# A two-layer streaming encoder step: the first two tiles of the pool projection taken together, and what is moved around them

## The chip, the cores and the metric

The kernel runs on one core of a Trainium2 chip. The time is the device time in microseconds (us) of one execution. Engines are named as in the profile: PE (TensorE, matmuls; PEld its weight loads), DVE (VectorE), ACT (ScalarE), POOL (GpSimd), SP (SyncE, which issues most DMA transfers).

## What is computed

Two layers over 512 prompt rows and 32 sample rows (544 rows, kept as columns), width 2048, all in fp32. Layer 0 is attention; the change touches its last stage and the whole of layer 1, the pool mixer:

```python
mod = (cond @ w_ada[i] + b_ada[i])[:, None, :]        # cond = silu(c)
shift, scale, gate = jnp.split(mod, 3, axis=-1)
h = _rmsnorm(x, g_norm[i]) * (1 + scale) + shift
...
u, gate = jnp.split(h @ w_in, 2, axis=-1)             # the pool projection, 2048 -> 4096
u_ext = jnp.concatenate([prefix, u], axis=1)
# four channel groups: trailing means over 2, 4, 8, 16 rows, minus u  -> d
m = einsum(d, w_grp) * scale
y = (m * jax.nn.silu(gate)) @ w_out
x = x + gate_mod * y
```

## The kernel before

**Tiles.** A projection is done in tiles of 128 output channels. A tile's weights are 128 x 2048 fp32 (1 MB). They are loaded into one of two slots of `w_raw`, and DVE splits them in two instructions into an upper part `w_hi` (L1607) and a lower part `w_lo` (L1608); this is `split(g)`, for the tile with the running number g. PE multiplies upper by upper, upper by lower, and lower by upper part of `h`, 16 blocks of 128 input channels, each block three products on two halves of the 544 columns: 96 matmuls of 272 columns a tile, accumulated in the PSUM slot `g % 2` (two banks). Tile g may be split when tile g-2 has been multiplied, and its raw weights may be loaded when tile g-2 has been split. `big_wait` is PE's wait for the split and for the free PSUM slot, `big_tile` the 96 matmuls.

**Pool projection.** There are 32 such tiles, `G_PIN` to `G_PIN + 31`, called pool tile 0 to 31 here. Even ones give 128 channels of `u`, odd ones the matching gate channels. `u_and_gate(t)` on ACT evicts tile 2t into `u_ext`, and tile 2t+1 through silu to `stage` and to DRAM. DVE forms the trailing means of tile 2t in between (L2015 and the lines behind it, here the pool work), and ACT stores them (`d_scr`).

**Modulation on DVE.** The vector `cond @ w_ada` is made partly by DVE: `ada_tile(a)` multiplies a 1 MB tile of `w_ada` with the broadcast condition `cond_b` (two instructions L1645) and counts `adr_used`. Sixteen of these tiles (modulation tile 0 to 15 here) are left for the pool projection: one per pool tile in the loops t = 0 to 7. They all go through one buffer, `w_adr[:, 1]`, so SP may load modulation tile k only when tile k-1 has been used. SP works in order, and its instructions are waits and issues: for each t it issued the weights of pool tiles 2t and 2t+1, and then modulation tiles 2t and 2t+1 (L641 to L646).

**Between the layers.** The last tiles of the attention's output projection (`G_O2 + 14`, `G_O2 + 15`) go PE, ACT (`gated`: eviction L1510, then square L1203), DVE (`update` L1976, x + gate * y), POOL (L715, sum of squares). After the last one PE sums over the partitions (`row_sums(1)`), DVE and ACT make 1/rms (`row_scale`, L1582, L1587, L1209), and `make_h1` on DVE with `affine1` on ACT makes the 16 blocks of `h` (L1618, L1231, L1626), one after the other; `h_ready` counts them. PE took pool tile 0 block by block as they came (`big_tile` with `h_wait`), and then tile 1. ACT made `silu` of `cond_b` (L1525) behind `affine1`, and DVE's loop starts with a wait for it, and then `split(G_PIN + 1 + 2t)`.

**Loop of DVE before**, for each t: split of tile 2t+1, modulation tile 2t, pool work, split of tile 2t+2, modulation tile 2t+1, a wait for the store of the means. After t = 15 comes the group stage (`G_GRP`, four 512 x 512 maps) and the last projection (`G_POUT`).

## Time and profile before

| | us |
|---|---|
| median of 3 runs | 2057.33 (2054.09 to 2057.75) |
| the profiled execution, its time | 2055.34 |
| its span | 2053.6 |
| PE busy | 1842.7 (90%) |
| DVE busy | 1257.0 (61%) |
| ACT busy | 413.7 (20%) |
| mean granted TensorE clock | 0.944 of full speed |

The times of the trace count from the start of the span, of which 1.7 us of the execution's time lie outside. The trace lists consecutive instructions of one form as one row; "idle before" in square brackets is what the engine waited before the row, and for whom.

### The profile page before, as it was taken

To read this page: it belongs to the slowest core of one execution; us is meant where nothing else is said; L and a number is where in the kernel's file an instruction comes from. 1 tells how busy PE (TensorE), PEld (TensorE's weight loads), DVE (VectorE), ACT (ScalarE), POOL (GpSimd) and SP (SyncE) were. 2 spreads that over 40 slices of the span, in tenths; PEclk is the share of its full clock that TensorE was granted. 3 is DMA by queue.
4 is the path that set the end of the run, shared out by engine and by line. 5 is a ranking of instruction groups with operands and counts; after the bars stand their busy time and mean duration, and the time that the engine had idled before them with its cause. 6 is when DMAs were issued, how large, how long until landed. Compare 5 with 4: busy or idle time off the path is not lost.

```text
span 2053.6 us, 32706 instructions
## 1 busy us (share of the span) xinstructions
PE 1842.7 (90%) x13182; PEld 1702.1 (83%) x13182; DVE 1257.0 (61%) x1601; ACT 413.7 (20%) x914; POOL 198.1 (10%) x117
## 2 busy tenths in 40 slices
PE   4548999999999999997888889959999999999995
PEld 0108999999999997776777779958999999999995
DVE  4898766776876674553555544377777544574444
ACT  1241000000010113331455533440000000121111
POOL 2770000000600000000000011200000000001110
PEclk8878999999999999999799998979999999999997
DMA  9664554554655532205333253304455332552222
GB/s 387 233 225 175 203 208 185 206 210 185 234 192 211 193 135 62 75 15 164 99 117 117 87 207 128 96 37 169 182 185 202 118 113 103 179 186 82 82 82 87
DMA packets 86106, 316.07 MB, mean 154 GB/s; under 512 B 12184, under 2 KB 20552, under 8 KB 60448
## 3 DMA queue, kind: packets, MB, share of 16 engines
q1 hardware_dynamic: 64208, 237.70, 32.0%
q10 hardware_dynamic: 21200, 76.48, 10.4%
q0 software_dynamic: 640, 1.10, 0.2%
q8 instruction: 38, 0.62, 0.1%
q14 instruction: 20, 0.16, 0.0%
HBM read 282.56 MB, written 32.69 MB: 154 GB/s over the span
## 4 chain that ended last, share of the span: by engine, by line
PE 69%; DVE 12%; DMA 6%; issue 5%; ACT 4%; POOL 2%; SPq 0%; DVEq 0%; ACTq 0%; POOLq 0%
PE banks L732 68%; DVE banks L1645 3%; DMA w_raw<-in_w_pin 3%; POOL ssq L690 2%; DMA w_adr<-in_w_ada_dve 2%; DMA w_more<-in_w_ada_pe 2%; ACT pxd L1428 1%; DVE std L1884 1%; DVE w_hi L1607 1%; DVE h_lo L400 1%; DVE rstd L1587 1%; DVE x L2083 1%; ACT px L1346 0%; DVE pt_lo L1818 0%; DVE w_hi L1868 0%
## 5 line engine op out<-in xcount | busy, mean ns | idle before, releaser
L732 PE MATMUL banks<-h_hi,w_hi 128*128 128x272 f32 x3968 | 831.4, 295 | 61.2 <-DVE w_lo L1608 29.6
L732 PE MATMUL banks<-h_lo,w_hi 128*128 128x272 f32 x3712 | 778.3, 292 | 0.0
L732 PE MATMUL banks<-h_hi,w_lo 128*128 128x272 f32 x3456 | 722.8, 291 | 0.0
L732 PEld LDWEIGHTS banks<-h_hi,w_hi 128*128 128x128 f32 x3968 | 635.4, 194 | 70.3 <-issue 47.8
L732 PEld LDWEIGHTS banks<-h_lo,w_hi 128*128 128x128 f32 x3712 | 596.5, 193 | 0.0
L732 PEld LDWEIGHTS banks<-h_hi,w_lo 128*128 128x128 f32 x3456 | 547.6, 192 | 0.0
L1645 DVE CUSTOM_DVE_ANT_0 banks<-w_adr,cond_b 128x2048 f32<-128x2048 f32 x160 | 386.2, 2414 | 20.2 <-DMA w_adr<-in_w_ada_dve 17.0
L1607 DVE CAST w_hi<-w_raw 128x2048 fp32r<-128x2048 f32 x101 | 125.6, 1244 | 223.4 <-PE banks L732 171.5
L1608 DVE TENSOR_TENSOR w_lo<-w_raw,w_hi 128x2048 fp32r<-128x2048 f32 x101 | 249.2, 2467 | 3.5
L1280 ACT ACTIVATE stage<-banks 128x544 f32<-128x544 f32 x46 | 28.9, 629 | 495.6 <-PE banks L732 495.6
L1976 DVE TENSOR_TENSOR x<-x,stage 128x544 f32 (+1 forms) x32 | 23.9, 748 | 171.0 <-ACT stage L1510 171.0
L715 POOL TENSOR_TENSOR ssq<-ssq,stage 128x544 f32<-128x544 f32 x32 | 49.9, 1560 | 751.0 <-ACT stage L1203 751.0
L732 PE MATMUL banks<-w_more,cond_t 128*2 128x512 f32 x80 | 40.6, 661 | 38.1 <-DMA w_more<-in_w_ada_pe 21.2
L1510 ACT ACTIVATE stage<-banks,mod 128x272 f32<-128x272 f32 (+2 forms) x96 | 32.6, 410 | 202.3 <-PE banks L732 202.3
L732 PEld LDWEIGHTS banks<-w_more,cond_t 128*2 128x2 f32 x80 | 6.7, 90 | 70.6 <-issue 44.0
L732 PE MATMUL banks<-w_raw,cond_t 128*2 128x512 f32 x48 | 31.2, 812 | 32.8 <-DMA w_raw<-in_w_ada_pe 32.8
L2015 DVE TENSOR_TENSOR w<-u_ext 128x573 f32<-128x573 f32 x16 | 12.1, 756 | 69.6 <-ACT u_ext L1535 68.6
L732 PEld LDWEIGHTS banks<-w_raw,cond_t 128*2 128x2 f32 x48 | 4.5, 103 | 57.8 <-DMA w_raw<-in_w_ada_pe 30.5
L1540 ACT ACTIVATE stage<-banks 128x544 f32<-128x544 f32 x16 | 10.0, 626 | 186.6 <-PE banks L732 186.6
L1428 ACT ACTIVATE pxd<-banks,std 128x128 f32<-128x128 f32 (+3 forms) x64 | 33.2, 524 | 64.8 <-DVE std L1885 41.0
L721 POOL TENSOR_TENSOR cos_t<-cos_t,kpe 128x544 f32<-128x544 f32 x8 | 10.8, 1346 | 343.4 <-ACT kpe L1400 343.4
L1932 DVE TENSOR_TENSOR ptd_lo<-banks,ptd_hi 128x128 fp32r<-128x128 f32 (+3 forms) x32 | 15.7, 492 | 43.3 <-ACT ptd_hi L1450 43.3
(301 smaller groups left out, 1703.8 us busy)
## 6 DMA issues: line engine op xcount, KB each, us to landing
w_adr<-in_w_ada_dve ACTq DMA_DIRECT2D x46, 1024.0 KB, 4.9
w_adr<-in_w_ada_dve SPq DMA_DIRECT2D x34, 1024.0 KB, 4.9
w_raw<-in_w_z SPq DMA_DIRECT2D x32, 1024.0 KB, 5.9
w_raw<-in_w_pin SPq DMA_DIRECT2D x32, 1024.0 KB, 5.9
w_raw<-in_w_gate SPq DMA_DIRECT2D x16, 1024.0 KB, 7.0
w_raw<-in_w_out SPq DMA_DIRECT2D x32, 512.0 KB, 3.9
w_raw<-in_w_pout SPq DMA_DIRECT2D x16, 1024.0 KB, 4.9
w_more<-in_w_ada_pe SPq DMA_DIRECT2D x10, 1024.0 KB, 7.4
```

Of the source, the lines that this page charges most:

```text
L400: ins = eng.scalar_tensor_tensor(out=h_lo[:, k, r], in0=x[:, k, r], scalar=mod[:, c, k:k + 1], in1=h_hi[:, k, r].bitcast(F32), op0=ALU.add ...
L690: pool.tensor_tensor(ssq[:], ssq[:], (stage[:, 0], rstd[:])[k % 2], ALU.add).then_inc(sq_added, 1)
L715: pool.tensor_tensor(ssq[:], ssq[:], stage[:, s], ALU.add).then_inc(sq_added, 1)
L732: return pe.matmul(out, lhsT, rhs, start=start, stop=stop)
L1280: act.activation(rows(stage[:, s]), acc[slot], func).then_inc(acc_free[slot], 1)
L1428: ins = act.activation(pxd[:, w % 3, e, 0:n], PS[:, 2 * (w % 2) + e, 0:n], ACT.Exp, bias=std[:, w, 2 + e:3 + e], scale=DIFF_SCALE, accum_o ...
L1510: ins = act.activation(stage[:, s, r], PS[:, 2 * slot + bank, cols], ACT.Identity, scale=mod[:, c, bass.ds(2 * t + (gate_tile + s), 1)])
L1587: vchain(dve, dve.reciprocal(rstd[:], rstd[:]))
L1607: vchain(dve, dve.tensor_copy(w_hi[:, slot], w_raw[:, slot]))
L1608: dve.tensor_tensor(w_lo[:, slot], w_raw[:, slot], w_hi[:, slot].bitcast(F32), ALU.subtract).then_inc(split_ready, 1)
L1645: ins = dve.tensor_tensor_reduce(ada_junk, w_adr[:, slot if buf is None else buf], cond_b[:, c, :], 1.0, 0.0, ALU.mult, ALU.add, ada_acc[: ...
L1976: dve.tensor_tensor(at(x, t2 + k), at(x, t2 + k), stage[:, slot], ALU.add).then_inc(x_new, 1)
```

## The change

PE takes pool tiles 0 and 1 together: for each of the 16 blocks of `h` the products of tile 0 and then of tile 1. For this the weights of tile 1 are split earlier, between `fold_scale` and `row_scale`. All later splits of DVE's loop move by one tile: at t it now splits tile 2t+2 first, and tile 2t+3 behind the pool work; the last two of these (t = 15) are the weights of groups 0 and 1, and the group stage splits one group further ahead. SP loads the weights of pool tiles 0 and 1 first and then, for each t, modulation tile 2t, weights of tile 2t+2, modulation tile 2t+1, weights of tile 2t+3. The silu of `cond_b` stands on ACT ahead of the last two `gated` steps of the attention instead of behind `affine1`. The first tile of layer 0 (`G_KPE`) is only written out, with the same instructions.

```diff
--- before.py
+++ after.py
@@ -638,13 +638,14 @@
                     sp.wait_ge(split_ready, 2 * t + 2 + G_O2 - G_KPE + s)
                     sp.dma_start(w_raw[:, (G_O2 + s) % 2, 0:D // 2],
                                  tile_of(wo2, s, t + 1)[:, 0:D // 2]).then_inc(raw_in[(G_O2 + s) % 2], 16)
+            for s in range(2):
+                load_w(w_pin[s], (G_PIN + s) % 2, G_PIN - G_KPE + s)
             with sp.Fori(0, KT // 2) as t:
-                for s in range(2):
-                    load_w(tile_of(wp2, s, t), (G_PIN + s) % 2, 2 * t + G_PIN - G_KPE + s)
                 for s in range(2):
                     sp.wait_ge(adr_used, 2 * t + (ADA_P0 + ADA_P1 + s))
                     sp.dma_start(w_adr[:, 1], tile_of(wd2, s, t + (ADA_P0 + ADA_P1) // 2)).then_inc(adr_in[s], 16)
-            with sp.Fori(KT // 2, KT) as t:
+                    load_w(tile_of(wp2, s, t + 1), (G_PIN + s) % 2, 2 * t + G_PIN + 2 - G_KPE + s)
+            with sp.Fori(KT // 2 + 1, KT) as t:
                 for s in range(2):
                     load_w(tile_of(wp2, s, t), (G_PIN + s) % 2, 2 * t + G_PIN - G_KPE + s)
             sp.wait_ge(adr_used, ADA_P0 + ADA_P1 + KT)
@@ -778,10 +779,8 @@
                                   first and i == 0, last and i == 2)
                 return m
 
-            def big_tile(slot, h_wait=None):
+            def big_tile(slot):
                 for k in range(KT):
-                    if h_wait is not None:
-                        pe.wait_ge(h_ready, h_wait + k + 3)
                     m = tile_products(slot, k, k == 0, k == KT - 1)
                 m.then_inc(mm_done, 1)
 
@@ -800,7 +799,10 @@
             ada_turn(CHUNKS - 1)
 
             big_wait(G_KPE)
-            big_tile(G_KPE % 2, 0)
+            for k in range(KT):
+                pe.wait_ge(h_ready, k + 3)
+                m = tile_products(G_KPE % 2, k, k == 0, k == KT - 1)
+            m.then_inc(mm_done, 1)
             big_loop(G_Z, 0, ZT // 2)
             big_loop(G_GATE, 0, GT // 2 - 1)
             big_wait(G_GATE + GT - 2)
@@ -1153,7 +1155,12 @@
             row_sums(1)
             for s in range(2):
                 big_wait(G_PIN + s)
-                big_tile((G_PIN + s) % 2, KT)
+            for k in range(KT):
+                pe.wait_ge(h_ready, KT + k + 3)
+                for s in range(2):
+                    m = tile_products((G_PIN + s) % 2, k, k == 0, k == KT - 1)
+                    if k == KT - 1:
+                        m.then_inc(mm_done, 1)
             big_loop(G_PIN, 1, KT)
             for g in range(4):
                 slot = (G_GRP + g) % 2
@@ -1517,12 +1524,12 @@
 
             with act.Fori(0, KT // 2 - 1) as t:
                 gated(t, G_O2, 1, 2 * KT, halves=True)
+            act.wait_ge(condb_in, 32)
+            act.activation(cond_b[:], cond_b[:], ACT.Silu).then_inc(condb_ready, 1)
             with act.Fori(KT // 2 - 1, KT // 2) as t:
                 gated(t, G_O2, 1, 2 * KT)
             root(1)
             affine1()
-            act.wait_ge(condb_in, 32)
-            act.activation(cond_b[:], cond_b[:], ACT.Silu).then_inc(condb_ready, 1)
 
 
             act.wait_ge(pad_zero, 1)
@@ -1991,6 +1998,7 @@
                     split(G_PIN)
             dve.memset(lam_in[:, 0, 0:1], 0.0).then_inc(pad_free, 1)
             fold_scale(1)
+            split(G_PIN + 1)
             row_scale(1)
             make_h1()
 
@@ -2003,7 +2011,7 @@
                     t0 = t - 4 * grp
                     dv.loop(t0, 2 + grp + 1 + 1 + 1 + (4 if grp < 2 else 0))
                     dve_t2 = 2 * t
-                    split(G_PIN + 1, dve_t2, t)
+                    split(G_PIN + 2, dve_t2, t)
                     if grp < 2:
                         ada_tile(ADA_P0 + ADA_P1, dve_t2, t, 1)
                     dve.wait_ge(acc_free[us], t + turn_of(G_PIN + 2))
@@ -2025,7 +2033,7 @@
                     dve.tensor_copy(last[:, 0, :], u_ext[:, NP:PAD + NP])
                     vchain(dve, dve.tensor_copy(last[:, 1, :], u_ext[:, PAD + R:2 * PAD + R]))
                     dve.memset(lam_in[:, 0, 0:1], 0.0).then_inc(d_ready, 1)
-                    split(G_PIN + 2, dve_t2, t)
+                    split(G_PIN + 3, dve_t2, t)
                     if grp < 2:
                         ada_tile(ADA_P0 + ADA_P1 + 1, dve_t2, t, 1)
                     dve.wait_ge(d_stored, 16 * t + 16)
@@ -2059,12 +2067,13 @@
             lower_d(0)
             dve.wait_ge(pg_stored, 16 * KT)
             for g in range(4):
-                split(G_GRP + g + 1)
                 group_out(4 * g)
                 if g < 3:
                     lower_d(g + 1)
                 for n in range(1, 4):
                     group_out(4 * g + n)
+                if g < 3:
+                    split(G_GRP + g + 2)
                 dve.memset(lam_in[:, 0, 0:1], 0.0).then_inc(acc_free[(G_GRP + g) % 2], 1)
             group_out(KT)
 
```

On SP's queue, in the loop over the first eight t, this stood before (a repetition issues two weight tiles, then two modulation tiles):

```order
L641 ISA
L482 ISA [waits split_ready]
L482 DMA w_raw<-in_w_pin 128x2048
L481 REGISTER_ALU
L482 ISA [waits split_ready]
L482 DMA w_raw<-in_w_pin 128x2048
L645 REGISTER_ALU
L646 ISA [waits adr_used]
L646 DMA w_adr<-in_w_ada_dve 128x2048
L645 REGISTER_ALU
L646 ISA [waits adr_used]
L646 DMA w_adr<-in_w_ada_dve 128x2048
```

and this stands there now:

```order
L646 ISA [waits adr_used]
L646 DMA w_adr<-in_w_ada_dve 128x2048
L481 REGISTER_ALU
L482 ISA [waits split_ready]
L482 DMA w_raw<-in_w_pin 128x2048
L645 REGISTER_ALU
L646 ISA [waits adr_used]
L646 DMA w_adr<-in_w_ada_dve 128x2048
L481 REGISTER_ALU
L482 ISA [waits split_ready]
L482 DMA w_raw<-in_w_pin 128x2048
L643 REGISTER_ALU
```

Each of the two weight issues now stands behind a wait on `adr_used` of its own. On DVE, at the end of the attention, this stood before (the last `update` steps, `pad_free`, `fold_scale`, `row_scale`):

```order
L1976 TENSOR_TENSOR x<-x,stage 128x544 [waits acc_free1]
L1607 CAST w_hi<-w_raw 128x2048 [waits mm_done,raw_in1]
L1608 TENSOR_TENSOR w_lo<-w_raw,w_hi 128x2048 [waits dve_step]
L1976 TENSOR_TENSOR x<-x,stage 128x544 [waits acc_free0]
L1992 MEMSET lam_in 128x1
L1598 SCALAR_TENSOR_TENSOR aff<-mod,gnorm_t 128x16 x2
L1582 TENSOR_SCALAR rstd<-banks 128x544 [waits var_ready,dve_step]
```

and this stands there now:

```order
L1983 TENSOR_TENSOR x<-x,stage 128x544 [waits acc_free1]
L1614 CAST w_hi<-w_raw 128x2048 [waits mm_done,raw_in1]
L1615 TENSOR_TENSOR w_lo<-w_raw,w_hi 128x2048 [waits dve_step]
L1983 TENSOR_TENSOR x<-x,stage 128x544 [waits acc_free0]
L1999 MEMSET lam_in 128x1
L1605 SCALAR_TENSOR_TENSOR aff<-mod,gnorm_t 128x16 x2
L1614 CAST w_hi<-w_raw 128x2048 [waits mm_done,raw_in0,dve_step]
L1615 TENSOR_TENSOR w_lo<-w_raw,w_hi 128x2048 [waits dve_step]
L1589 TENSOR_SCALAR rstd<-banks 128x544 [waits var_ready]
```

The split of tile 1 has come in ahead of the instruction that reads the row sums. On ACT this stands now between the loop of `gated` and its last two steps (a table load and the silu, which were behind `affine1`), and a table load for the square root has come in behind them:

```order
L1528 ACT_TABLE_LOAD
L1528 ACTIVATE cond_b<-cond_b 128x4096
L1529 UNCONDITIONAL_BRANCH
L1517 ACTIVATE stage<-banks,mod 128x272
L1517 ACTIVATE stage<-banks,mod 128x240
```

The silu now stands ahead of the evictions of the attention's last two tiles. The loop of `u_and_gate`, which had no table load before, now has one ahead of the copy of `pool_pre` (L1538) and one ahead of the silu of the gate tile (L1547).

## Rows read from the trace of the kernel before

**Rows 1.** The page: the chain that ended last, shares of the span by engine.

```profile
PE 69%; DVE 12%; DMA 6%; issue 5%; ACT 4%; POOL 2%; SPq 0%; DVEq 0%; ACTq 0%; POOLq 0%
```

**Rows 2.** Waits of PE, 1240 to 1700 us: us in total, times, longest.

```profile
PE banks L732 <- DVE w_lo L1608: 17.9, 8, 5.3
```

**Rows 3.** Timeline of PE: start us, us, instruction, idle before.

```profile
1356.34 0.79 PE L732 MATMUL banks<-h_hi,w_hi 128*128 128x272 f32 x2 [9.09 <-DVE h_lo L1626]
...
1382.02 0.41 PE L732 MATMUL banks<-h_hi,w_lo 128*128 128x272 f32 x2
1387.69 0.82 PE L732 MATMUL banks<-h_hi,w_hi 128*128 128x272 f32 x2 [5.26 <-DVE w_lo L1608]
...
1404.03 0.52 PE L732 MATMUL banks<-h_hi,w_hi 128*128 128x272 f32 x2 [2.16 <-DVE w_lo L1608]
```

**Rows 4.** Timeline of DVE between the layers.

```profile
1338.08 3.34 DVE L1608 TENSOR_TENSOR w_lo<-w_raw,w_hi 128x2048 fp32r<-128x2048 f32 x1
1342.19 0.73 DVE L1976 TENSOR_TENSOR x<-x,stage 128x544 f32<-128x544 f32 x1 [0.77 <-ACT stage L1510]
...
1347.36 0.72 DVE L1582 TENSOR_SCALAR rstd<-banks 128x544 f32<-128x544 f32 x1 [4.26 <-PE banks L732]
...
1378.34 1.74 DVE L1626 SCALAR_TENSOR_TENSOR h_lo<-w,mod,h_hi 128x512 f32 x4
```

**Rows 5.** Timeline of POOL between the layers.

```profile
1337.68 1.59 POOL L715 TENSOR_TENSOR ssq<-ssq,stage 128x544 f32<-128x544 f32 x1 [3.94 <-ACT stage L1203]
1343.68 1.33 POOL L715 TENSOR_TENSOR ssq<-ssq,stage 128x544 f32<-128x544 f32 x1 [4.41 <-ACT stage L1203]
```

**Rows 6.** Timeline of ACT between the layers.

```profile
1331.20 0.66 ACT L1203 ACTIVATE stage<-x 128x544 f32 x1
1335.13 1.02 ACT L1510 ACTIVATE stage<-banks,mod 128x272 f32<-128x272 f32 x3 [3.27 <-PE banks L732]
...
1378.78 1.28 ACT L1525 ACT_TABLE_LOAD   x1
1380.07 3.62 ACT L1525 ACTIVATE cond_b<-cond_b 128x4096 f32<-128x4096 f32 x1
```

**Rows 7.** Timeline of DVE in the loop, t = 1: modulation, pool work, split, modulation.

```profile
1417.04 2.30 DVE L1645 CUSTOM_DVE_ANT_0 banks<-w_adr,cond_b 128x2048 f32<-128x2048 f32 x1
...
1427.38 1.23 DVE L1607 CAST w_hi<-w_raw 128x2048 fp32r<-128x2048 f32 x1 [5.28 <-DMA w_raw<-in_w_pin]
...
1433.24 2.30 DVE L1645 CUSTOM_DVE_ANT_0 banks<-w_adr,cond_b 128x2048 f32<-128x2048 f32 x1
```

**Rows 8.** The casts L1607, 1415 to 1600 us: what DVE waited for before them.

```profile
  DMA w_raw<-in_w_pin: 34.6, 7
```

**Rows 9.** Timeline of SP's DMA issues: weights of pool tiles 4 and 5, modulation tile 4.

```profile
1420.42 0.91 SPq L482 DMA_DIRECT2D w_raw<-in_w_pin  x2
1435.78 0.33 SPq L646 DMA_DIRECT2D w_adr<-in_w_ada_dve  x1
```

**Rows 10.** Modulation loads, 1400 to 1600 us: issue to landing, us.

```profile
DMA to landing us min/median/max: 4.8/4.9/5.9
```

**Rows 11.** Stretches: PE, PEld, DVE, ACT, POOL busy, then clock, DMA share, GB/s.

```profile
1421.50:1429.50 8.00, 8.00 (x66) 8.00 (x65) 2.58 (x7) 0.00 (x0) 0.00 (x0) 1.00 0.99 399
1387.60:1392.00 4.40, 4.31 (x19) 4.31 (x20) 4.37 (x4) 0.00 (x0) 0.00 (x0) 0.51 0.02 4
```

**Rows 12.** Timeline of ACT: evictions as pool tiles 2, 17 and 31 end.

```profile
1417.87 0.75 ACT L1535 ACTIVATE u_ext<-banks 128x272 f32<-128x272 f32 x3 [12.53 <-PE banks L732]
...
1612.12 0.63 ACT L1540 ACTIVATE stage<-banks 128x544 f32<-128x544 f32 x1 [11.28 <-PE banks L732]
...
1780.49 0.62 ACT L1540 ACTIVATE stage<-banks 128x544 f32<-128x544 f32 x1 [11.27 <-PE banks L732]
```

**Rows 13.** Timeline of DVE and PE as the group stage starts.

```profile
1782.49 2.63 DVE L2039 TENSOR_TENSOR h_lo<-d_raw,h_hi 128x544 fp32r<-128x544 f32 x4 [5.07 <-ACT h_hi L1557]
...
1783.36 0.49 PE L732 MATMUL banks<-h_hi,w_hi 128*128 128x272 f32 x2 [2.91 <-DVE h_lo L2039]
```

## The prediction, made before the result was known

> **What bounds the kernel now.** I read the page first (its chain of work that ended last), then the waits of PE in the second half, then the timelines of all engines from the end of the attention to the group stage. The chain is 69% PE [rows 1], so what can be won or lost is PE's idle time and its slow clock. Around the change there are two kinds. Between the layers PE waits 9.09 us for the first block of `h`, takes tile 0 as the blocks come, ends it at 1382.4 and then waits 5.26 us for the split of tile 1, which stands behind the silu of `cond_b` [rows 3]. And in the loop PE waits for splits: 17.9 us in 8 waits, the 5.26 and one of 2.16 among them [rows 2, 3].
>
> The reader should see why the loop waits. From tile 2's start at 1404.0 to tile 17's end at 1612.1 pass 208.1 us for 16 tiles; from tile 17's end to tile 31's, without modulation, 14 tiles take 168.4 us, 12.03 each [rows 3, 12]. Sixteen tiles at 12.03 are 192.5, so 15.6 us are lost to the loop. DVE is not short of time; it waits for DMA: 34.6 us before seven casts, all of them of even tiles [rows 8]. The reason is SP's order. Modulation tile k may be loaded only when k-1 has been used, and what stands behind that wait on SP waits too. In t = 1 the second product of modulation tile 2 ends at 1419.34 (1417.04 + 2.30) [rows 7]; only then do modulation tile 3 and, at 1420.42, the weights of tiles 4 and 5 go out [rows 9], and DVE casts tile 4 at 1427.38, 8.04 us after that end, of which 5.28 idle and the rest pool work [rows 7]. Tile 5's weights came in the same volley, so its split waits for no DMA. One exposed load per two tiles: that is the old pattern.
>
> **Part 1, the pass by block.** PE's wait of 9.09 us stays. Blocks of `h` come from 1356.3 to 1380.1 (1378.34 + 1.74), 1.7 us apart on average [rows 3, 4]; two tiles need 12/96 of 12.03 us, 1.50 us a block, at full clock, and about twice that at half clock. At 0.51 PE ran for some 4.4 us after the 5.26 us wait [rows 11]; I take the same after 9.09 us. PE then falls about two blocks behind and catches up at 0.2 us a block; it ends both tiles some 2 to 3 us after the last block, tile 0 at about 1382.4 as before and tile 1 at 1383. Tile 2 then is where tile 1 was.
>
> **Part 2, silu two steps forward.** ACT is free at 1331.86 (1331.20 + 0.66); table load and silu take 1.28 + 3.62 [rows 6], to 1336.8. The eviction that started at 1335.13 slips by 1.7 us. DVE had 0.77 us of slack before the last update [rows 4], so the last update, square and row sums slip by 0.9 us. The table load for the square root (1.28) hides: ACT had over 3 us until the sums were ready at 1347.36 [rows 4]. So do the two table loads that each repetition of `u_and_gate` now has: ACT is idle 11.3 to 12.5 us before an eviction [rows 12].
>
> **Part 3, split of tile 1 under the row sums.** From 1344.1 (1342.19 + 0.73 + 0.9 and `fold_scale`, 0.3): 1.23 for the cast and 2.3 to 3.34 for the lower part (3.34 beside a POOL addition [rows 4, 5]), end 1347.6 to 1348.7; the sums are ready at 1348.3 at the earliest. POOL's addition took 1.59 beside the earlier split and 1.33 alone [rows 5]; I add up to 0.5. Parts 2 and 3 together move `h` by 1.4 us (bounds 0.9 and 2.4). The cover is thin here and is used up.
>
> The Trainium skill, "SBUF — State Buffer", section "Who interferes with whom", has the port pair of DVE and GpSimd as an exclusive lock that a cast, too, can hold. By that rule POOL's last addition (now due at 1344.6) would stand still until the cast ends at 1345.3, and the sum would be 0.3 us more. The 3.34 us row agrees with a lock; the POOL row, 1.59 against 1.33, is near to it.
>
> So tile 0 ends at 1383.8, the split of tile 2 (which waits for that, and for nothing else now that silu is early and its weights are loaded) runs 1383.85 to 1387.4, and PE starts tile 2 at 1387.5 after an idle gap of 3 us. Before it started it at 1404.0. **Up to here the change wins 16.5 us.** Modulation tile 0 has been used at 1383.85 + 8.16 = 1392.0. (8.16: from a cast at 1427.38 to the end of the second product at 1433.24 + 2.30 [rows 7].)
>
> **Part 4, the new order of loads and splits.** This is the large term. SP now has modulation tile k+1 and directly behind it the weights of tile k+3; both sit behind the wait for the use of modulation tile k. DVE now has, in order: modulation tile k, (pool work), split of tile k+3, modulation tile k+1. So *every* split of tiles 3 to 17 starts a load after the modulation tile before it: one exposed load per tile, 15 of them, where there was one per two tiles. It is a closed chain on DVE and DMA: use of k, issue, load, split, use of k+1.
>
> Its price a tile: the load link, where pool work stands in it and the store of the means runs beside it, is the old one: mean idle 4.94 (34.6/7) and pool work of 2.7 to 3.5, 8.1 us [rows 7, 8]. Where none stands in it: issue 0.24 after the end (1435.54 to 1435.78) [rows 7, 9], modulation landing 4.9 [rows 10], the 1.05 MB of weights behind it 2.6 at 399 GB/s [rows 11], 7.7 us. Mean 7.9; with the 8.16 on DVE a tile takes **16.1 us** against PE's 12.03 (or 13.8 with a slow start, below). Pool work hides in the link, PE's own time too, since the split of tile k+3 needs only tile k+1.
>
> From the use of tile 0 at 1392.0, 14 periods to the use of tile 14: 1617.4; link 8.1 and split 3.5: tile 17 can start at 1629.1. Tile 2 took 13.8 us after a gap of 2.16 us, as the clock fell in it [rows 3, 12]; the gaps are 2.3 us now, so tile 17 takes 13.8 too and ends at 1642.9. Before: 1612.1 [rows 12]. **Plus 30.8 us**, the 16.5 already counted. Behind it tile 18 waits for nothing (its load follows tile 17's at once, its split ends about 1640.5), and both kernels run at 12.03 a tile to tile 31.
>
> The Trainium skill, "TensorE: Matmul & The Clock Gate", section "HAM oscillation — how this bites in real kernels", says that a wait for DMA between short pieces of matmul work makes each piece start at the lower clock. By that each of these 15 tiles loses about 1.8 us (13.8 against 12.03), but the sum moves only by the last one, already in it, as DVE and DMA are late by more.
>
> **Part 5, group stage.** The split of group 1 used to stand behind the first `lower_d`; now it stands between the end of tile 31 (1780.45) and it: 3.5 us and the loop's end, some 0.5. `lower_d` started 2.0 us after that end [rows 12, 13], now 4.0; PE's wait of 2.91 grows by 1.9 us. What it saves (`group_out` 0 earlier) is on no engine that PE waits for. Bounds 1.0 and 2.5.
>
> **Sum.** 2055.3 (profiled execution) + 30.8 + 1.9 = 2088.0. The median of the runs is 2.0 above that execution; I forecast **2089 us**. Own range: the link, 15 times. Low end -0.5 each (weights landing at the highest rate, no d store beside), high end +0.6 (modulation landing at 5.9 in some [rows 10]): -8, +9; parts 1 to 3 -1, +3; runs 2. That gives 2078 to 2102.
>
> **Rivals.** *Faster, period kept:* the volley of two weight tiles survives in effect, and the loop goes on at 26.0 us for two tiles (208.1/16 x 2). Then the 16.5 us stay won: 2055.3 - 16.5 + 1.9, 2041. It decides by whether the odd tile's weights can go out before the even modulation tile is used; SP's order says no. 0.04. *Faster, bound by PE:* the link shrinks below 12.03 - 8.16 = 3.9 us, tiles 2 to 17 take 192.5 us, end 1580: 2055.3 - 32 + 1.9, 2025. A single modulation load takes 4.8 at least [rows 10]. 0.03. *Slow clock all through:* with gaps before each tile the clock stays at the lower level, a tile takes about 22 us (96 matmuls at the 4.4 us for 19 of [rows 11]), PE is the bound: 16 x 22 from 1387.5 end at 1740, 128 us later than before, 2185. Against it: after a gap of 2.16 us tile 2 still took only 13.8. 0.03. *The change does not do what it says:* tile 1 is not ready when `h` comes, and PE holds back the pass: a few us more, inside the range. 0.05. *No change to measure:* would need gain and loss to cancel, a link of about 5.8 us; 0.02. The forecast itself has 0.83.
>
> Faster by over 0.2% (about what a measurement of this kernel can tell from no change) 0.06, within 0.02, slower 0.92. The range, 2076 to 2104, takes in the forecast's own and leaves out the rivals.
>
> **What would show it.** In the changed kernel: PE ends tiles 0 and 1 within 1 us of each other, about 1385, and starts tile 2 near 1387.5; casts of pool weights wait for DMA 15 times, not 7, 80 to 95 us in total; casts stand 16 us apart through tiles 3 to 17; PE waits for `w_lo` in each of them, some 35 us in total; tile 17 ends near 1643, tile 31 near 1811; PE waits 4.8 us before the group stage. The prediction is wrong if casts of odd tiles do not wait for DMA, or if tile 17 ends before 1630.

## The result and the profile after

| | before | changed | ratio |
|---|---|---|---|
| median, us | 2055.71 (2053.0 to 2057.75) | 2097.2 (2093.4 to 2100.99) | 1.0203, interval [1.0178, 1.0227] |
| profiled execution, us | 2055.34 | 2093.4 | |
| its span | 2053.6 | 2091.6 | |
| granted clock, mean | 0.944 | 0.940 | |

The kernel became 2% slower; 2089 was forecast (range 2076 to 2104). Medians are over the executions in the faster of the two states; an execution of 9950 us of the kernel with the weights first (below) and one of 3039 us of the kernel before are not among them. Lines of the changed kernel are 7 or 8 higher. The chain that ended last, to be read beside [rows 1]; DMA has gone from 6% to 8% and PE from 69% to 67%:

```profile
PE 67%; DVE 13%; DMA 8%; issue 5%; ACT 4%; POOL 2%; SPq 1%; DVEq 0%; ACTq 0%; POOLq 0%
```

**An offset first.** Already ahead of the first changed instruction this trace runs late: the square on ACT that began at 1331.20 before [rows 6] begins at 1333.74, 2.54 us later, in code that the change does not touch. So the offset of 2.5 us is taken off wherever a time of after is set against one of before. It lies within the scatter between executions: in the eleven profiled executions of this study the first product of the row sums starts between 1345.1 and 1350.2, and two kernels below that are alike up to there have it at 1345.95 and at 1350.18.

**Between the layers.** ACT, then POOL's last addition, then DVE (start us, us, instruction, idle before):

```profile
1333.74 0.66 ACT L1210 ACTIVATE stage<-x 128x544 f32 x1
1334.41 1.28 ACT L1528 ACT_TABLE_LOAD   x1
1335.71 3.63 ACT L1528 ACTIVATE cond_b<-cond_b 128x4096 f32<-128x4096 f32 x1
1339.24 1.00 ACT L1517 ACTIVATE stage<-banks,mod 128x272 f32<-128x272 f32 x3
```

```profile
1346.89 1.86 POOL L716 TENSOR_TENSOR ssq<-ssq,stage 128x544 f32<-128x544 f32 x1 [3.56 <-ACT stage L1210]
```

```profile
1346.34 1.23 DVE L1614 CAST w_hi<-w_raw 128x2048 fp32r<-128x2048 f32 x1
1347.60 3.30 DVE L1615 TENSOR_TENSOR w_lo<-w_raw,w_hi 128x2048 fp32r<-128x2048 f32 x1
1351.03 0.72 DVE L1589 TENSOR_SCALAR rstd<-banks 128x544 f32<-128x544 f32 x1
```

The read of the sums was at 1347.36 [rows 4] and is at 1351.03: 3.67, less the offset 1.2 us. POOL's last addition takes 1.86 us instead of 1.33 [rows 5], since it now lies beside the split. Then PE; the first row is the row sums' products, which waited 3.96 us in before:

```profile
1348.81 2.18 PE L733 MATMUL banks<-ssq,ones 128*128 128x272 f32 x4 [5.16 <-POOL ssq L716]
1360.12 0.79 PE L733 MATMUL banks<-h_hi,w_hi 128*128 128x272 f32 x2 [9.12 <-DVE h_lo L1633]
...
1386.63 0.41 PE L733 MATMUL banks<-h_hi,w_lo 128*128 128x272 f32 x2
1390.01 0.51 PE L733 MATMUL banks<-h_hi,w_hi 128*128 128x272 f32 x2 [2.98 <-DVE w_lo L1615]
```

DVE casts tile 2 at 1386.33, as tile 0 is done; PE ends tile 1 at 1387.0 and starts tile 2 at 1390.01, less the offset 1387.5. In before that was 1404.03 [rows 3]. The 16.5 us are there, and then they are lost.

**The loop.** What the casts of the pool weights waited for from 1380 to 1700 us, and PE's waits for the lower part from 1240 to 1710 us (us in total, times, longest), to be read beside [rows 8] and [rows 2]:

```profile
  DMA w_raw<-in_w_pin: 96.5, 15
```

```profile
PE banks L733 <- DVE w_lo L1615: 46.5, 16, 4.9
```

Two turns of the closed chain: SP's issues, the stores of ACT in the first turn, and the casts of DVE that end each load:

```profile
1394.71 0.33 SPq L646 DMA_DIRECT2D w_adr<-in_w_ada_dve  x1
1395.29 0.33 SPq L482 DMA_DIRECT2D w_raw<-in_w_pin  x1
1412.47 0.33 SPq L646 DMA_DIRECT2D w_adr<-in_w_ada_dve  x1
1413.06 0.33 SPq L482 DMA_DIRECT2D w_raw<-in_w_pin  x1
1428.52 0.33 SPq L646 DMA_DIRECT2D w_adr<-in_w_ada_dve  x1
```

```profile
1397.43 0.37 ACTq L1545 DMA_DIRECT2D pool_d_scratch<-d_st  x1
...
1399.85 0.36 ACTq L1549 DMA_DIRECT2D pool_gate_scratch<-stage  x1
```

```profile
1404.08 1.23 DVE L1614 CAST w_hi<-w_raw 128x2048 fp32r<-128x2048 f32 x1 [6.82 <-DMA w_raw<-in_w_pin]
...
1420.13 1.23 DVE L1614 CAST w_hi<-w_raw 128x2048 fp32r<-128x2048 f32 x1 [7.53 <-DMA w_raw<-in_w_pin]
```

The time from a modulation tile's issue to the cast I call the link; from the cast to the next issue it is always 8.39 us. A link is called even or odd by the modulation tile before it, the one whose use released it. The even ones hold the pool work and the two stores; they take 8.60 us in the mean of the first seven (9.37, 8.64, 8.83, 8.54, 8.26, 8.37, 8.21; the eighth, at the end of the chain, 7.87). The odd ones take 7.53 (7.66, 7.81, 7.46, 7.49, 7.40, 7.44, 7.47). So a tile takes 17.0 and 15.9 us in turn, where PE's work is 12.03.

**The end of the loop and the group stage**: ACT evicts tile 18 and the last tile; PE begins the groups (it waited 2.91 us there in before [rows 13]):

```profile
1660.98 0.75 ACT L1542 ACTIVATE u_ext<-banks 128x272 f32<-128x272 f32 x3 [4.78 <-PE banks L733]
...
1817.32 0.62 ACT L1547 ACTIVATE stage<-banks 128x544 f32<-128x544 f32 x1 [11.28 <-PE banks L733]
```

```profile
1821.66 0.79 PE L733 MATMUL banks<-h_hi,w_hi 128*128 128x272 f32 x2 [4.37 <-DVE h_lo L2047]
```

Tile 17 ended 12.03 before the first of these, at 1648.9. The last tile ends 36.8 us later than in before [rows 12], 34.3 without the offset.

### The profile page after: what moved, and what is told of

Its sections match the earlier page's. It is cut to its first block, busy times and chain, and to the rows that moved or that the text cites. A ratio compares the mean times of both kernels' runs of the same rounds, so it can differ in the third digit from the quotient of the medians.

```text
span 2091.6 us, 32744 instructions
## 1 busy us (share of the span) xinstructions
PE 1857.9 (89%) x13182; PEld 1714.9 (82%) x13182; DVE 1256.3 (60%) x1601; ACT 452.3 (22%) x945; POOL 199.4 (10%) x117
## 4 chain that ended last, share of the span: by engine, by line
PE 67%; DVE 13%; DMA 8%; issue 5%; ACT 4%; POOL 2%; SPq 1%; DVEq 0%; ACTq 0%; POOLq 0%
PE banks L733 66%; DMA w_raw<-in_w_pin 5%; DVE banks L1652 4%; POOL ssq L691 2%; DMA w_more<-in_w_ada_pe 1%; DVE w_hi L1614 1%; ACT pxd L1435 1%; DMA d_raw<-pool_d_scratch 1%; DVE std L1891 1%; DVE h_lo L400 1%; DVE rstd L1594 1%; DVE x L2092 1%; DVE w_lo L1615 0%; ACT px L1353 0%; DVE pt_lo L1825 0%
## 5 line engine op out<-in xcount | busy, mean ns | idle before, releaser
L1287 ACT ACTIVATE stage<-banks 128x544 f32<-128x544 f32 x46 | 28.8, 626 | 492.9 <-PE banks L733 492.9
L695 POOL TENSOR_TENSOR x<-x,rstd 128x544 f32<-128x544 f32 x16 | 41.2, 2609 | 11.2 <-DVE ada_acc L1688 11.2
```

Of the source, the lines that this page charges most:

```text
L695: pool.tensor_tensor(x[:, k], x[:, k], rstd[:], ALU.mult).then_inc(x_normed, 1)
L1287: act.activation(rows(stage[:, s]), acc[slot], func).then_inc(acc_free[slot], 1)
```

## The experiments

Every kernel was measured beside the kernel before on the same chip, and ratios are to that. Where traces are compared I count from the start of the row sums' products (`ssq,ones`) to the end of the span: 708.5 us in before (2053.6 - 1345.07), 742.8 in the changed kernel. That takes the offset out. It does not take out all scatter: the profiled execution lies 3.8 us below the median of the changed kernel, and up to 5.2 us away from it in others. A difference of a few us between two totals is therefore followed to the stretch where it arises.

### The queue order alone

**Changed kernel, weights ahead of the modulation tile.** Only SP's queue is edited:

```diff
                 for s in range(2):
+                    load_w(tile_of(wp2, s, t + 1), (G_PIN + s) % 2, 2 * t + G_PIN + 2 - G_KPE + s)
                     sp.wait_ge(adr_used, 2 * t + (ADA_P0 + ADA_P1 + s))
                     sp.dma_start(w_adr[:, 1], tile_of(wd2, s, t + (ADA_P0 + ADA_P1) // 2)).then_inc(adr_in[s], 16)
-                    load_w(tile_of(wp2, s, t + 1), (G_PIN + s) % 2, 2 * t + G_PIN + 2 - G_KPE + s)
```

> The changed kernel with one edit on SP's queue: in the loop over t the weights of pool tile 2t+2+s are issued ahead of the wait for modulation tile 2t+s-1's use and of modulation tile 2t+s's load, not behind them. Theory (queue order): the weights then are in flight a whole tile early, no cast of tiles 3 to 17 waits for DMA, and PE is the bound at 12.03 us a tile from tile 2 on. Tile 17 ends about 32 us before that of the kernel before, 65 us before that of the changed kernel; time near 2025, ratio to the kernel before 0.985. Rival (DVE's order): split and modulation tile in one row on DVE delay the splits whatever SP does; then the casts keep a distance near 16 us and the time stays near 2090. Rival (clock): PE's clock stays low after the gaps; the time falls only part of the way.

Measured: 2025.5 us, ratio 0.984, interval [0.980, 0.988]; 677.1 us from the row sums on, 65.7 less than the changed kernel. The casts of pool weights from 1380 to 1700 us no longer wait for DMA at all, but for PE to finish the tile whose slot they write:

```profile
  PE banks L733: 92.0, 24
```

```profile
1387.00:1650.00 263.00, 260.02 (x2068) 259.81 (x2067) 190.02 (x228) 46.37 (x80) 0.00 (x0) 0.99 0.48 171
```

This row is the stretch of the loop (PE, PEld, DVE, ACT, POOL busy, clock, DMA share, GB/s): PE is busy 260.0 of 263 us. In the changed kernel it is

```profile
1387.00:1650.00 263.00, 216.45 (x1547) 213.24 (x1547) 159.95 (x195) 32.38 (x57) 0.00 (x0) 0.92 0.40 148
```

Two lines of SP's queue make the difference between 2% slower and 1.6% faster. All that part 4 of the prediction priced hangs on them.

**Kernel before, with that order.** The same interleaving in the kernel before, nothing else (the loop behind starts one t later, as in the changed kernel):

```diff
+            for s in range(2):
+                load_w(w_pin[s], (G_PIN + s) % 2, G_PIN - G_KPE + s)
             with sp.Fori(0, KT // 2) as t:
                 for s in range(2):
-                    load_w(tile_of(wp2, s, t), (G_PIN + s) % 2, 2 * t + G_PIN - G_KPE + s)
-                for s in range(2):
+                    load_w(tile_of(wp2, s, t + 1), (G_PIN + s) % 2, 2 * t + G_PIN + 2 - G_KPE + s)
                     sp.wait_ge(adr_used, 2 * t + (ADA_P0 + ADA_P1 + s))
```

> The kernel before with the same order on SP's queue (weights of pool tiles 0 and 1 ahead of the loop, then for each t: weights 2t+2, modulation 2t, weights 2t+3, modulation 2t+1); DVE, PE and ACT as in the kernel before. Theory (queue order): the seven waits of DVE for weights (34.6 us idle) go, and with them the 15.6 us that PE loses between the start of tile 2 and the end of tile 17, less what the modulation load (4.9 us behind the use of the one before) still costs: 12 to 15 us faster, near 2042, ratio 0.993. Rival (DVE's order or the volume of DMA bounds the loop of the kernel before): no change, ratio 1.000.

Measured: 2037.1 us, ratio 0.990 [0.987, 0.993]. From the row sums on it is 19.6 us less than before, where 12 to 15 were expected. From tile 1's start to the last tile's end PE needs 375.1 us (1388.86 to 1763.93) where before took 392.8 (1387.69 to 1780.49): 17.7 us, which is the 15.6 us that the prediction read from the loop and the wait of 2.16 us ahead of it [rows 3]. Nothing of it is left to the modulation loads, for which the expectation had taken some off. Another 1.8 us came in the group stage, for a reason that has nothing to do with the edit (below, under the group stage).

### The pass by block alone

```diff
-            for k in range(KT):
-                pe.wait_ge(h_ready, KT + k + 3)
-                for s in range(2):
+            for s in range(2):
+                for k in range(KT):
+                    pe.wait_ge(h_ready, KT + k + 3)
                     m = tile_products((G_PIN + s) % 2, k, k == 0, k == KT - 1)
-                    if k == KT - 1:
-                        m.then_inc(mm_done, 1)
+                m.then_inc(mm_done, 1)
```

Tile 0 takes the blocks as they come and tile 1 follows, all else as in the changed kernel:

> The changed kernel, but PE takes tile 0 over all blocks and then tile 1, as before; everything else changed. Theory: in the changed kernel the chain of DMA, split and modulation bounds the loop, and its start (split of tile 2) waits only for tile 0, which ends at the same time either way, so the pass by block is worth nothing there: same time as the changed kernel within 3 us (tile 1 now ends some 12 us later, still before the split of tile 3, due 20 us after tile 0's end). Rival: the pass is worth its 12 us also here, and this kernel takes 12 us more than the changed one.

Measured: 2090.5 us, ratio 1.015 [1.012, 1.018]; from the row sums on 744.6 us against 742.8. No gain of the pass shows here. The ratios have this kernel 0.5% faster without it, with intervals that barely overlap. Of the 1.8 us that its trace is longer, 1.3 arise behind the last pool tile, where the same wait (4.38 us) was followed by a granted clock of 0.50 for 4 us instead of 0.64. The chain itself is not helped by the pass: its last cast, of tile 17, starts 283.1 us after the row sums without it and 284.1 with it. And the same in the kernel with the weights first:

> The first kernel of this set (weights ahead of modulation on SP's queue), and PE takes tile 0 and then tile 1. Theory: with the chain gone PE is the bound, and the pass by block is worth tile 1's 12 us less the gap of 3 us that it leaves before tile 2 (in its place tile 2's split lies under tile 1): 8 to 10 us slower than the kernel with weights first and the pass, near 2034. Rival (the pass is worth a full tile or nothing): 12 or more, or 0.

Measured: 2032.0 us, 0.988 [0.985, 0.991], where 8 to 10 us above the kernel with the pass were expected. The medians are 6.5 us apart, though the intervals of the two ratios overlap; the traces say 683.8 against 677.1, 6.6 us. Here tile 1 ends at 1394.85, 48.9 us after the row sums, and tile 2 follows at once; with the pass tile 2 starts after 41.2, 7.7 us earlier. One us of it is given back, as PE's granted clock was 0.65 for the 4 us behind its wait of 2.98 us. So the pass is a gain of 6.6 us that shows only where the loop behind it is bound by PE; in the changed kernel tile 1's early end meets a chain of DVE and DMA that does not wait for it.

### The silu alone

```diff
             with act.Fori(0, KT // 2 - 1) as t:
                 gated(t, G_O2, 1, 2 * KT, halves=True)
+            act.wait_ge(condb_in, 32)
+            act.activation(cond_b[:], cond_b[:], ACT.Silu).then_inc(condb_ready, 1)
```

(and out of its place behind `affine1`), in the kernel before:

> The kernel before with one part of the change: the conditions' silu stands ahead of ScalarE's last O2 step and no longer behind the last products of h. It prices that part alone. Theory: at the front it costs what the changed kernel's trace shows there (row sums 1.2 us later by the sums' read, once the 2.5 us that the whole trace ran late are taken off), and it frees what the trace of before shows as VectorE's wait for it, 4.00 us ahead of the cast at 1384.08; tile 1's low parts, for which TensorE waits 5.3 us there, come 2.5 to 2.8 us earlier. If tile 2's start hands this on down the loop, the time is 2 to 3 us below before, near 2053 for a before of 2056; the cast at 1384.08 stands near 1381.5. Rival: the loop behind is paced by its transfers, whose issues hang on SP's modulation tiles and not on tile 1, and the lead is eaten at the first wait for a raw tile (5.28 us): then the time is within 1 us of before, and the cast at 1427.38 stands where it was.

Measured: 2052.9 us, ratio 0.9979 [0.9969, 0.9988]. PE's wait ahead of the row sums is 4.63 us, 0.67 more than 3.96. The cast that waited 4.00 us for `cond_b` does so no more; in before and here:

```profile
1384.08 1.23 DVE L1607 CAST w_hi<-w_raw 128x2048 fp32r<-128x2048 f32 x1 [4.00 <-ACT cond_b L1525]
```

```profile
1381.83 1.23 DVE L1607 CAST w_hi<-w_raw 128x2048 fp32r<-128x2048 f32 x1 [0.32 <-DVE h_lo L1626]
```

From the row sums on it takes 704.7 us, 3.8 less than before; less the 0.67 in front the move is worth 3.1 us. The lead is handed on to the end of the last pool tile (431.6 us after the row sums, 435.4 in before), as the theory said.

### Why the even link is longer

The prediction had 16.3 us for such a tile, the trace 17.0. First, the gate tile's eviction and store are moved ahead of ScalarE's wait for `d`:

```diff
-                act.wait_ge(d_ready, t + 1)
-                act.dma_start(d_scr[bass.ds(t, 1)].rearrange("t p r -> p (t r)"), d_st[:]).then_inc(d_stored, 16)
                 act.wait_ge(mm_done, 2 * t + (G_PIN + 2))
...
                 act.dma_start(pg_scr[bass.ds(t, 1)].rearrange("t p r -> p (t r)"), stage[:, 1]).then_inc(pg_stored, 16)
+                act.wait_ge(d_ready, t + 1)
+                act.dma_start(d_scr[bass.ds(t, 1)].rearrange("t p r -> p (t r)"), d_st[:]).then_inc(d_stored, 16)
```

> The changed kernel, but ScalarE evicts and stores the gate tile ahead of its wait for d and of d's store (the SP queue is as in the changed kernel). It asks why two tiles take 32.9 us where 32.2 were forecast: the link behind a gate tile (odd) lasts 15.9 us as forecast, the other (even) 17.0 instead of 16.3. Theory: the gate tile's store (128 x 544) leaves some 2.4 us after d's store and both run beside the modulation tile and the weight tile, which share 295 to 313 GB/s there against 399 where they are alone; with the gate store ahead, one of the two stores leaves the stretch in which the two 1 MB tiles are in flight. Then the even links are 16.3 to 16.6 us, two tiles take 32.2 to 32.5 us, and the time is 3 to 5 us below the changed kernel (near 2093 for 2097). Rival: the even link is longer because VectorE and not the transfer comes late, or because the stores share the stretch in either order: links of 17.0 us again and a time within 1 us of the changed kernel.

Measured: 2096.9 us, ratio 1.0192 [1.0175, 1.0210]; 740.9 us from the row sums on. The even link takes 8.33 us (mean of seven), 0.27 less, and not the 0.4 to 0.7 expected: the gate store was a third of it. The kernel without the pass, whose stores are those of the changed kernel, has 8.54 in the same mean, so such a mean is good to about 0.1. The 1.9 us of the trace are 7 x 0.27, and too small for the medians to show. Then the store of `d` too is held until tile 2t+3 is split:

```diff
                 act.wait_ge(d_ready, t + 1)
+                act.wait_ge(split_ready, 2 * t + (G_PIN + 5 - G_KPE))
                 act.dma_start(d_scr[bass.ds(t, 1)].rearrange("t p r -> p (t r)"), d_st[:]).then_inc(d_stored, 16)
```

> The changed kernel with ScalarE's gate store ahead of the store of d (as in e6_gate_store_first), and the store of d held until VectorE has split tile 2t+3, so that neither store leaves ScalarE while the modulation tile and the weight tile are in flight. From the issue of the modulation tile to the cast, even links took 8.60 us in the changed kernel and 8.33 with the gate store moved, odd ones 7.53 and 7.52. Theory: what is left of the difference, 0.8 us, is the store of d (272 KB, 6.4 us from issue to landing, beside the two 1 MB tiles); then even links take 7.5 to 7.6 us like the odd ones, two tiles 31.8 to 31.9 us instead of 32.9, and from the start of the row sums' products to the end the program takes near 735 us (742.8 in the changed kernel, 740.9 in e6_gate_store_first); a median near 2089 for the changed kernel's 2097. Rival: even links are longer for another reason (VectorE's pool work standing ahead of the cast, the same bytes only in another order): they stay at 8.2 to 8.4 us. Second rival: the store, now behind the split, lands too late for VectorE's wait for it at the end of the loop's body, and the odd links grow instead.

Measured: 2088.6 us, ratio 1.016 [1.014, 1.018]. A link with both kinds of store out of it; SP, DVE and ACT's store:

```profile
1425.76 0.33 SPq L646 DMA_DIRECT2D w_adr<-in_w_ada_dve  x1
1426.34 0.33 SPq L482 DMA_DIRECT2D w_raw<-in_w_pin  x1
1441.68 0.33 SPq L646 DMA_DIRECT2D w_adr<-in_w_ada_dve  x1
```

```profile
1433.29 1.23 DVE L1615 CAST w_hi<-w_raw 128x2048 fp32r<-128x2048 f32 x1 [4.99 <-DMA w_raw<-in_w_pin]
```

```profile
1436.88 0.35 ACTq L1550 DMA_DIRECT2D pool_d_scratch<-d_st  x1
```

The pool work still stands ahead of the cast, and the link is 7.53 us, like the odd ones. So are the five behind it (7.45 to 7.50); the first of the seven is still 8.59 with no store in it, and why is open. What made the other even links longer than the odd ones was the stores beside the loads, with 0.27 us for the gate's and some 0.8 for that of `d`. The changed kernel's own links agree: in its turns two to four `d` is stored 2.7 us after the modulation tile's issue and the even link takes 8.67 us in the mean; in the last four the pool work is longer, `d` is stored after 3.5 us, and the links take 8.18. The store felt it as well, 272 KB from issue to landing (line, KB each, median us), in the changed kernel and here:

```profile
pool_d_scratch<-d_st ACTq DMA_DIRECT2D x7, 272.0 KB, 6.4
```

```profile
pool_d_scratch<-d_st ACTq DMA_DIRECT2D x7, 272.0 KB, 2.1
```

The median is 8.6 us below that of the changed kernel, as forecast, but the trace does not bear that size out: from the row sums on it takes 741.0 us and not the 735 expected. The last pool tile does end 5.7 us earlier (462.8 after the row sums, 468.5 in the changed kernel), but then PE waits for the group stage:

```profile
1816.58 0.79 PE L733 MATMUL banks<-h_hi,w_hi 128*128 128x272 f32 x2 [6.89 <-DVE h_lo L2048]
```

6.89 us instead of 4.37: the last `d` too is stored behind a split (at 1813.37, 3.65 us after the last eviction began), and the group stage loads it back. The next group begins 15.27 us later, not 13.88: the granted clock behind that wait is 0.50 for 4 us, 0.64 in the changed kernel. Together 3.9 us of the 5.7 are gone again.

### The group stage's split, and a version with all three

The split of group 1 behind the first `lower_d`, as it was before, in the kernel with the weights first (the loop's last repetition is written as a loop of its own for this):

```diff
-                    split(G_PIN + 3, dve_t2, t)
+                    if first_t < 15:
+                        split(G_PIN + 3, dve_t2, t)
...
             dve.wait_ge(pg_stored, 16 * KT)
+            split(G_GRP + 1)
             for g in range(4):
```

> The changed kernel with the weight tile issued ahead of the modulation tile (as in e1_weights_first) and the split of the group stage's second weight tile back where the kernel before had it: behind the last group's first part and the wait for the gate stores, and not inside the last loop. It prices what the changed split order costs at the start of the group stage. Theory: VectorE's 3.5 us of cast and subtraction for that tile stand ahead of the first group's products of d; TensorE waits 4.4 us there in the changed kernel and 2.9 us in before; so the wait falls to near 2.9 us and the time to 1.5 to 1.9 us below e1_weights_first, near 2025.6 for its 2027.3. Rival: the second tile is then late instead (TensorE needs it 12 us after the first), VectorE waits for the gate stores as in before, and the gain is below 0.5 us, or a loss.

Measured: 2025.6 us, ratio 0.985 [0.984, 0.986]. PE's wait is that of before again:

```profile
1756.05 0.49 PE L733 MATMUL banks<-h_hi,w_hi 128*128 128x272 f32 x2 [2.91 <-DVE h_lo L2049]
```

405.9 us after the row sums against 407.4 in the kernel without this edit: 1.5 us, as expected. The medians cannot show it: 2025.6 here and 2025.5 without the edit, each on a chip of its own, and ratios of 0.985 and 0.984. And with the silu between the root and the products of `h`:

```diff
             root(1)
+            act.wait_ge(condb_in, 32)
+            act.activation(cond_b[:], cond_b[:], ACT.Silu).then_inc(condb_ready, 1)
             affine1()
```

> As e8_group_back, and the silu between the root and the products of h, where ScalarE sat idle 5.1 us: ahead of the last O2 step it delays that step's eviction. Theory: the silu with its table load (4.9 us) fits into that gap nearly whole; the 1.2 us that the silu costs at the row sums come back less the 0.3 to 0.5 us that stay through GpSimd's slower add beside VectorE, and the time is 0.7 to 1.2 us below e8_group_back. From the start of the row sums' products to the end of the program the times should be those of e8_group_back within 0.5 us, and TensorE's wait ahead of the row sums near 4.4 us instead of 5.2. Rival: a table load of 1.28 us more, for the root and silu alternate, pushes the first products of h: TensorE's wait behind the row sums grows from 9.1 to over 9.6 us and the time is that of e8_group_back or up to 1 us above.

Measured: 2027.2 us, ratio 0.986 [0.985, 0.988], not to be told from the one before it. The step itself did what was said: PE waits 4.49 us for the row sums where it waited 5.20, and 9.13 before `h` in both, and tile 2 starts 41.2 us after the row sums in both. So the 0.7 to 1.2 us expected are 0.7 in that wait, below what the medians show, and another term covers them. After the same wait of 2.91 us PE's clock for the first 4 us of the group stage was 1.00 in the one and 0.64 in the other:

```profile
1756.10:1760.10 4.00, 4.00 (x32) 4.00 (x33) 3.97 (x5) 0.62 (x2) 0.00 (x0) 1.00 0.26 48
```

```profile
1751.30:1755.30 4.00, 4.00 (x22) 4.00 (x23) 3.97 (x5) 0.63 (x2) 0.00 (x0) 0.64 0.28 39
```

Group 0 took 12.54 us in the first and 13.87 in the second, with the same instructions. The same holds for 1.5 of the extra 1.8 us of the kernel before with its weights first (its group 0 took 12.57 us, in before 14.10).

## Why the prediction was right

The time was 2097 for 2089, on the side and by the mechanism forecast. The size is less close than that looks: the medians moved by 41.5 us, the traces by 38.1, and the prediction's sum was 32.7. Its steps, with the offset of 2.5 us taken off:

- **Parts 1 to 3.** `h` later by 1.2 us for 1.4. The experiments split it: 0.67 is the silu (4.63 against 3.96), 0.53 is POOL's addition beside the split (1.86 against 1.33; the last kernel, with the silu away but the split in place, waits 4.49, 0.53 more than before). Tile 2 starts at 1387.5, as forecast; tiles 0 and 1 end 0.7 us apart, at 1386.3 and 1387.0 in the trace. The Trainium skill, "SBUF — State Buffer", section "Who interferes with whom", has DVE and GpSimd exclude each other on a shared port pair; POOL's addition began 0.68 us before the cast beside it ended, and 0.68 + 1.33 is 2.01, so the trace (1.86) is within 0.15 us of that.
- **Part 4, the chain.** One exposed load per tile, 15 waits for DMA, 96.5 us; 80 to 95 was said. The order theory was tested by undoing that order alone, and all 15 waits went. The part on DVE with the issue, priced at 8.16 + 0.24 = 8.40, is 8.39; a tile with an odd link takes 7.53 + 8.39 = 15.9, as priced.
- **The term that was mis-sized** is the even link: "the old one", 8.1 us with the issue, so 7.9 from the issue on. It was 8.60. The working took the link of before over as it was, so that a tile with such a link was priced at 16.3 us and took 17.0; in before the gate store did not fall into it (in the first turn it leaves at 1402.56, 2.2 us after the cast at 1400.34). Of the 0.7 us the gate store accounts for 0.27 (the run that moves it alone); where the rest comes from, with the store of `d` beside the loads before and after, no run here settles. The first link, 9.37 us, is long for a reason of its own, as it is 8.59 with no store in it. The stretch 1395 to 1404 moved 295 GB/s with two loads and two stores, where [rows 11] show 399 with three loads in flight. Seven such links are some 5 us. Modulation tile 15, which waits for the use of tile 14, goes out at 1622.6 (1625.07 less the offset) where 1617.4 + 0.24 was forecast: 4.9 us. The high end of the prediction's own range, +0.6 for each of 15 links, had this in it.
- **Tile 17** took 12.3 us (1636.62 to 1648.95) and not 13.8: -1.5, and by luck. Its gap was 1.2 us and not 2.3, but a gap of that size did not decide it either: of the six tiles behind gaps of 2.1 to 2.8 us three took 13.8 and three 12.3. It ends at 1646.4 for 1642.9 forecast. PE's waits for `w_lo` are 46.5 us for some 35. Of these, 2.98 stand ahead of tile 2; the rest of the difference is the longer links, a longer first gap (3.94 us) and the tiles, which took 13.5 us in the mean and not 13.8.
- **Part 5.** The wait of 2.91 became 4.37, 1.5 us more and not 1.9; moving the split back gives 1.46.
- **The sum**: 4.9 - 1.5 - 0.4 is 3.0 more than forecast, and with the offset of 2.5 us 2088.0 becomes 2093.5; the profiled execution took 2093.4. That is an account made afterwards, with the offset taken from the trace. The median of the runs lies 3.8 above it. The four executions took 2093.4, 2095.9, 2098.5 and 2101.0 us at mean granted clocks of 0.940, 0.939, 0.938 and 0.934; this is scatter between executions that no step of the working covers. In the prediction the way from 2088.0 to 2089 is not the 2.0 us that it names, its high end adds up to 2103 and not 2102, and its two faster rivals have 0.07 together where it says 0.06; nothing hangs on these.
- **The rivals.** "Bound by PE", 2025 us, is what the change gives with the two lines of SP's queue exchanged: 2025.5. The prediction gave it 0.03, since a modulation load takes 4.8 us at least. Those loads still take 4.9 us (median) there; what changed is that no split waits behind them. For the kernel as it was, the prediction's reading of SP's order held. The slow clock did not come: 0.92 in the loop.

The Trainium skill, "TensorE: Matmul & The Clock Gate", section "HAM oscillation — how this bites in real kernels", describes pieces of about 2 us of matmul work with waits of 3 to 5 us for DMA between them, and each piece starts at the lower clock. Here the pieces are tiles of 12 us. The trace agrees for gaps of that length: the seven tiles behind gaps of 3.1 to 4.9 us all took 13.6 to 15.1 us, with 12.03 at full clock. For shorter gaps it goes both ways: of the six tiles behind gaps of 2.1 to 2.8 us three took 13.8 and three 12.3, and at the group stage the same gap of 2.91 us cost 1.3 us in one kernel and nothing in another.

The fastest versions measured are the three with the weights ahead of the modulation tiles and the pass: 2025.5 us as it is, 2025.6 with the group split back, 2027.2 with the silu's third place as well. They cannot be told apart by medians; all are about 1.5% under before. Of the 31 us of the second against before, the order of SP's queue is worth 17.7 by the run that changes it alone, the pass 6.6, the silu 3.1, each measured in another kernel, so that adding them up is an estimate. What is left, some 4 us, no run isolates; that the 1.77 us for which PE still waits for tile 1's split in the kernel with the silu moved alone, and the full clock at the group stage (1.5 us), are most of it is not shown.

## What to carry to other kernels

In an in-order issue queue a transfer inherits every wait that stands ahead of it: before interleaving two streams of loads, ask of each issue which engine's progress the wait ahead of it hangs on, and put the stream whose wait is satisfied first in front. A chain "used, issue, load, split, used" closes as soon as both streams pass through one queue and one consumer, and its period is the sum of all its parts, whatever the engines' shares of busy time say. A gain ahead of such a chain (here the pass) is worth what the stage behind it can take, so fix the chain first and price the gain after.

## What the runs showed that was not expected

- A store of 272 KB that leaves beside two loads of 1 MB takes 6.4 us instead of 2.1, and makes the cast that waits for the second load some 0.8 us later (links of 8.33 and some 7.5 us). Held back until the split, it left the link as short as one without stores, but delayed the group stage at the end.
- The same wait of PE (2.91 us) is followed by a granted clock of 1.00 or of 0.64 for 4 us: 12.54 or 13.87 us for the same group of the group stage. Differences under 1.5 us between two traces should be read only up to such a place.
- ACT now loads a table twice in each repetition of its loop (1.28 us each time). PE waits for no instruction of ACT from 1376 to 1900 us in any kernel measured; but one of the loads stands ahead of the gate tile's eviction and so puts its store 1.3 us later, and what that does to the link no run here shows.
